# RWKV preparation reordered: small products first, decays beside the receptance, key norms per token

## What is computed

```python
xx = x_prev - x
r = (x + xx * mu[0]) @ w_rkv[0]
xw = x + xx * mu[1]
k = (x + xx * mu[2]) @ w_rkv[1]
v = (x + xx * mu[3]) @ w_rkv[2]
xa = x + xx * mu[4]
xg = x + xx * mu[5]
w_log = -softplus(-(w0 + tanh(xw @ w1) @ w2)) - 0.5
decay = exp(-exp(w_log))
a = sigmoid(a0 + (xa @ a1) @ a2)
g = sigmoid(xg @ g1) @ g2
kk = (k * k_k).reshape(B, S, H, N)
kk = kk / maximum(norm(kk, axis=-1), 1e-12)
k = k * (1.0 + (a - 1.0) * k_a)
# recurrence with state decay w, keys k, values v, removal -kk and kk * a
bonus = sum(rh * kh * r_k, axis=-1) * vh
```

## Time and profile before

| What | us |
|---|---|
| Median of 3 runs | 3485.09 |
| Lowest and highest run | 3481.71, 3485.85 |
| The profiled execution's own time | 3488.07 |
| Its span, first to last instruction | 3486.3 |
| TensorE busy | 3176.3 |
| VectorE busy | 1073.3 |
| ScalarE busy | 1038.5 |
| GpSimd busy | 751.4 |
| Mean granted TensorE clock | 0.946 of full speed |

### The profile page before, as it was taken

The page is one execution under the profiler, slowest core; times in us unless marked ns, Lnnn a source line. Parts: engine busy times, 40 slices in busy tenths (PEclk is TensorE's granted clock), DMA queues, the critical chain, the costliest instruction groups (busy, mean ns, idle before and its releaser), DMA issues.

```text
span 3486.3 us, 39216 instructions
## 1 busy us (share of the span) xinstructions
PE 3176.3 (91%) x16396; PEld 2264.3 (65%) x16396; DVE 1073.3 (31%) x1783; ACT 1038.5 (30%) x1775; POOL 751.4 (22%) x360
## 2 busy tenths in 40 slices
PE   7998999997885888888989999999999999999996
PEld 5676678885553888756768877777788574333332
DVE  4434320214277555653231022415230231000001
ACT  3533432324533221314343232431322031111110
POOL 3122244442220000003234443210144021100001
PEclk9999999998887888989999999999999999999998
DMA  3231143421110000032122322211132138999996
GB/s 113 91 127 61 49 170 108 145 97 36 61 49 1 2 2 2 14 97 91 51 82 97 97 85 97 85 49 49 37 97 88 63 154 367 409 399 413 417 415 274
DMA packets 217630, 447.75 MB, mean 128 GB/s; under 512 B 14176, under 2 KB 191360, under 8 KB 204528
## 3 DMA queue, kind: packets, MB, share of 16 engines
q1 hardware_dynamic: 197664, 389.04, 30.4%
q10 hardware_dynamic: 9744, 36.18, 2.6%
q0 software_dynamic: 10048, 20.02, 1.7%
HBM read 501.82 MB, written 31.46 MB: 153 GB/s over the span
## 4 chain that ended last, share of the span: by engine, by line
PE 80%; DVE 7%; DMA 6%; ACT 3%; issue 2%; POOL 1%; SPq 0%; ACTq 0%; POOLq 0%; DVEq 0%
PE product_banks L580 14%; PE product_banks L581 14%; PE product_banks L582 14%; PE product_banks L2130 7%; PE product_banks L548 5%; PE product_banks L2167 3%; DMA A<-in_w_down 3%; PE product_banks L663 3%; PE product_banks L2604 1%; PE score_banks L1159 1%; PE product_banks L622 1%; PE product_banks L623 1%; PE stat_bank L785 1%; PE stat_bank L701 1%; POOL Wr_parts L485 1%
## 5 line engine op out<-in xcount | busy, mean ns | idle before, releaser
L485 POOL TENSOR_TENSOR Wr_parts<-Wr,Wr_parts 128x1024 fp32r<-128x1024 f32 x202 | 487.1, 2413 | 1203.7 <-ACT Wr_parts L462 1203.7
L581 PE MATMUL product_banks<-A_parts,Wr_parts 128*128 128x512 f32 x1520 | 600.9, 395 | 0.0
L462 ACT ACTIVATE Wr_parts<-Wr 128x1024 fp32r<-128x1024 f32 x202 | 212.8, 1058 | 695.7 <-PE product_banks L582 632.1
L580 PE MATMUL product_banks<-H_parts,Wr_parts 128*128 128x512 f32 x840 | 341.9, 407 | 16.7 <-POOL Wr_parts L485 16.2
L2130 PE MATMUL product_banks<-A,Wr 128*64 128x512 f32 x1312 | 340.6, 597 | 3.4 <-DMA A<-in_w_up 2.2
L582 PE MATMUL product_banks<-H_parts,Wr_parts 128*128 128x512 f32 x840 | 334.2, 398 | 0.0
L581 PEld LDWEIGHTS product_banks<-A_parts,Wr_parts 128*128 128x128 f32 x1520 | 288.7, 190 | 66.3 <-issue 2.4
L485 POOL TENSOR_TENSOR shared_con_parts<-Wr,shared_con_parts 128x1024 fp32r<-128x1024 f32 x80 | 193.5, 2419 | 465.3 <-ACT shared_con_parts L462 465.3
L580 PE MATMUL product_banks<-A_parts,Wr_parts 128*128 128x512 f32 x680 | 268.3, 395 | 23.3 <-DVE A_parts L498 15.6
L582 PE MATMUL product_banks<-A_parts,Wr_parts 128*128 128x512 f32 x680 | 266.3, 392 | 0.0
L2130 PEld LDWEIGHTS product_banks<-A,Wr 128*64 128x64 f32 x1312 | 109.8, 137 | 209.2 <-issue 205.1
(11 more groups left out here) (480 smaller groups left out, 5067.6 us busy)
## 6 DMA issues: line engine op xcount, KB each, us to landing
A<-in_w_down SPq DMA_DIRECT2D x29, 2048.0 KB, 13.6
A<-in_w_gate SPq DMA_DIRECT2D x28, 2048.0 KB, 12.1
A<-in_w_up SPq DMA_DIRECT2D x28, 2048.0 KB, 16.9
Wr<-in_m_w_up SPq DMA_DIRECT2D x32, 1024.0 KB, 5.1
Wr<-in_m_w_down SPq DMA_DIRECT2D x32, 1024.0 KB, 4.9
Wr<-in_w_in SPq DMA_DIRECT2D x32, 1024.0 KB, 5.3
Wr<-in_c_w_kv SPq DMA_DIRECT2D x16, 1024.0 KB, 5.3
expert_rows<-LB ACTq DMA_DIRECT2D x12, 1024.0 KB, 4.0
```

The costliest lines, as they stand in the source:

```text
L462: nc.scalar.activation(weight_parts(s)[0], loaded_part(s), ACT.Copy).then_inc(*mark("weights_high", s))
L485: nc.gpsimd.tensor_tensor(lo, loaded_part(s), hi, ALU.subtract).then_inc(*mark("weights_split", s))
L580: pe.matmul(bank[:, :], hi[:, k, :], x_hi, start=(kk == 0), stop=False)
L581: pe.matmul(bank[:, :], hi[:, k, :], x_lo, start=False, stop=False)
```

## The change

The five small products come first, w1, a1, g1, w2, a2, and then r, k_ and v_ without anything between them, so that they form one run of split weights. The receptance's product is read by VectorE instead of ScalarE and multiplied by its decay in the same step. The decays are scanned before r. The running sum is kept, and the decay up to the token before is read as the neighbouring column instead of being made by a subtraction and an exponential of its own. ScalarE squares the keys straight out of the product's bank.

The key norms are kept per token: a sum for a tile is four matmuls of two columns (`kk_sum_pe`), ScalarE takes the root of 8 columns, VectorE works on 128 x 8 elements (`scale`), and TensorE spreads the scale over the channels again with eight matmuls of 128 columns (`kk_spread_pe`). `prepare` on VectorE finishes one tile of the keys. All this is written between the tiles of k_ and v_, as are the bonus sums and half of the values' turns. Eight bonus sums are copied out of their banks (`keep_sum`).

The core of the diff (removed lines can be seen in the functions above):

```diff
         if "B" in phases:
-            lin("r", a.b_w_rkv[0, 0], D, split=True)
             lin("w1", a.b_w1[0], 64)
+            lin("a1", a.b_a1[0], 64)
+            lin("g1", a.b_g1[0], 128)
             lin("w2", a.b_w2[0], D, k=64)
+            lin("a2", a.b_a2[0], D, k=64)
+            lin("r", a.b_w_rkv[0, 0], D, split=True, evac="dve")
             lin("k_", a.b_w_rkv[0, 1], D, split=True)
-            lin("a1", a.b_a1[0], 64)
-            lin("a2", a.b_a2[0], D, k=64)
...
-        MIX = [(0, "r"), (1, "w"), (2, "k"), (4, "a"), (5, "g"), (3, "v")]
-        LASTMM = {"r": ("r", 7), "w": ("w1", 0), "k": ("k_", 7), "a": ("a1", 0), "v": ("v_", 7),
-                  "g": ("g1", 0)}
+        MIX = [(1, "w"), (4, "a"), (5, "g"), (0, "r"), (2, "k"), (3, "v")]
+        MIX_AT = (48, 0, 16, 24, 8, 16)
...
+        def mix_high_act(act, m, t):
+            if m == 3:
+                act.wait_ge(*at("products_done", ("g1", 0)))
+            high_part(act, (("mix", m), t), MIX_PARTS[m](t)[0], mixbuf(m, t),
+                      [("mix_ready", (m, t))])
...
+            take(act, "w1", lambda j: LW[0:64, :], ACT.Tanh, n=1, rows=64)
             mix_act(act, 2)
+            take(act, "a1", lambda j: LB[0:64, 0, :], ACT.Copy, n=1, rows=64)
             mix_act(act, 3)
+            take(act, "g1", lambda j: LB[:, 1, :], ACT.Sigmoid, n=1)
+            for j in range(8):
+                mix_high_act(act, 3, j)
+                ps = take_product(act, "w2", j)
+                nc.scalar.activation(tile(48 + j), ps[:, :], ACT.Sigmoid, bias=pc("w0", j)).then_inc(
+                    *mark("products_read_by_act", ("w2", j)))
+            take(act, "a2", arena(32), ACT.Sigmoid, "a0")
+            first_highs(act, "r")
             mix_act(act, 4)
+            for j in range(8):
+                act.wait_ge(*at("scanned", j))
+                if j >= 2:
+                    act.wait_ge(*at("products_read_by_dve", ("r", j - 2)))
+                nc.scalar.activation(TMP[:, j % 2, :], tile(48 + j), ACT.Exp, scale=-DECAY).then_inc(
+                    *mark("first_decay_ready", j))
+                mix_high_act(act, 4, j)
+                take_product(act, "r", j)
             mix_act(act, 5)
...
+            def kk_root(j):
+                act.wait_ge(*at("kk_summed", j))
+                nc.scalar.activation(small[:, 48 + 8 * j:56 + 8 * j], B7[:, 8 * j:8 * j + 8],
+                                     ACT.Sqrt).then_inc(*mark("kk_root", j))
+            def decays(j):
+                act.wait_ge(*at("products_read_by_dve", ("r", 7)))
+                if j >= 2:
+                    act.wait_ge(*at("tilde_ready", j - 2))
+                nc.scalar.activation(TMP[:, j % 2, :], tile(48 + j), ACT.Exp, scale=DECAY).then_inc(
+                    *mark("decays_ready", (j, 0)))
+                nc.scalar.activation(tile(48 + j), tile(48 + j), ACT.Exp, scale=-DECAY).then_inc(
+                    *mark("decays_ready", (j, 1)))
+                act.wait_ge(*at("decays_ready", (j, 1)))
+                nc.scalar.activation(Pc[:, j, :], tile(48 + j)[:, CH - 1:T:CH], ACT.Copy).then_inc(
+                    *mark("chunk_decay_ready", j))
+            for j in range(8):
+                ps = take_product(act, "k_", j)
                 if j >= 2:
                     act.wait_ge(*at("kk_summed", j - 2))
+                nc.scalar.activation(SQ[:, j % 2, :], ps[:, :], ACT.Square,
+                                     scale=pc("k_k", j)).then_inc(*mark("kk_square", j))
+                nc.scalar.activation(tile(KT_ + j), ps[:, :], ACT.Copy).then_inc(
+                    *mark("products_read_by_act", ("k_", j)))
+                mix_high_act(act, 5, j)
+                if j:
+                    kk_root(j - 1)
+                if j >= 2:
+                    decays(j - 2)
...
+            for m, name in ((0, "w1"), (1, "a1"), (2, "g1")):
+                product(pe, name, *mixed(m))
+            product(pe, "w2", lambda k: LW[0:64, :], lambda k: [("products_read_by_act", ("w1", 0))])
+            product(pe, "a2", lambda k: LB[0:64, 0, :],
+                    lambda k: [("products_read_by_act", ("a1", 0))])
+            product(pe, "r", MIX_PARTS[3], low_ready(("mix", 3)))
+            def beside_keys(t):
+                if t:
+                    kk_sum_pe(pe, t - 1)
+                if t >= 2:
+                    kk_spread_pe(pe, t - 2)
+            product(pe, "k_", MIX_PARTS[4], low_ready(("mix", 4)), then=beside_keys)
+            def beside_values(t):
+                if t == 0:
+                    kk_sum_pe(pe, 7)
+                if t < 2:
+                    kk_spread_pe(pe, 6 + t)
+                else:
+                    bonus_sum_pe(pe, t - 2)
+                if t >= 4:
+                    value_turn_pe(pe, t - 4, 0)
+            product(pe, "v_", MIX_PARTS[5], low_ready(("mix", 5)), then=beside_values)
+            bonus_sum_pe(pe, 6)
+            for m in range(TT):
+                value_turn_pe(pe, m, 1)
+            bonus_sum_pe(pe, 7)
+            pe.wait_ge(*at("products_read_by_act", ("v_", 7)))
...
+        def kk_sum_pe(pe, j):
+            pe.wait_ge(*at("kk_square", j))
+            if j:
+                pe.wait_ge(*at("kk_root", j - 1))
             for m in range(TT):
+                mm = pe.matmul(B7[:, 8 * j + 2 * m:8 * j + 2 * m + 2],
+                               SQ[:, j % 2, m * P:(m + 1) * P], cc("blk")[:, 0:P:HD],
+                               start=True, stop=True)
+            mm.then_inc(*mark("kk_summed", j))
+        def kk_spread_pe(pe, j):
+            pe.wait_ge(*at("kk_scale_ready", j))
+            if j >= 2:
+                pe.wait_ge(*at("kk_ready", j - 2))
+            for m in range(TT):
+                for e in range(2):
+                    c = 48 + 8 * j + 2 * m + e
+                    mm = pe.matmul(S2[HD * e:HD * e + HD, j % 2, m * P:(m + 1) * P],
+                                   small[:, c:c + 1].broadcast_to([P, HD]), ident,
+                                   start=True, stop=True)
+            mm.then_inc(*mark("kk_spread", j))
+        def bonus_sum_pe(pe, j):
+            pe.wait_ge(*at("bonus_raw", j))
+            if j >= 2:
+                pe.wait_ge(*at("bonus_kept", j - 2))
+            else:
+                pe.wait_ge(*at("kk_ready", 6 + j))
+            pe.matmul(S2[:, j % 2, :], cc("blk"), SQ[:, j % 2, :], start=True, stop=True).then_inc(
+                *mark("bonus_summed", j))
...
             for j in range(8):
+                dve.wait_ge(*at("products_read_by_act", ("w2", j)))
+                nc.vector.tensor_tensor_scan(tile(48 + j), cc("reset"), tile(48 + j), 0.0,
+                                             ALU.mult, ALU.add).then_inc(*mark("scanned", j))
+            mix_dve(dve, 4)
+            for j in range(8):
+                ps = await_product(dve, "r", j)
+                dve.wait_ge(*at("first_decay_ready", j))
+                nc.vector.tensor_tensor(tile(RT_ + j), ps[:, :], TMP[:, j % 2, :], ALU.mult).then_inc(
+                    *mark("products_read_by_dve", ("r", j)))
+                mix_low_dve(dve, 4, j)
+            mix_dve(dve, 5)
+            def scale(j):
+                dve.wait_ge(*at("kk_root", j))
+                v = small[:, 48 + 8 * j:56 + 8 * j]
+                link(dve, nc.vector.tensor_scalar(v, v, 1e-12, None, ALU.max))
+                link(dve, nc.vector.reciprocal(v, v))
+                nc.vector.tensor_scalar(v, v, -1.0, None, ALU.mult).then_inc(
+                    *mark("kk_scale_ready", j))
+            KN = LB[:, 0, :]
+            def prepare(j):
+                k, b, e = tile(KT_ + j), tile(BT_ + j), tile(48 + j)
+                dve.wait_ge(*at("kk_spread", j))
                 dve.wait_ge(*at("products_read_by_act", ("k_", j)))
+                if j:
+                    dve.wait_ge(*at("a_tilde", j - 1))
+                nc.vector.scalar_tensor_tensor(out=KN, in0=k, scalar=pc("k_k", j),
+                                               in1=S2[:, j % 2, :], op0=ALU.mult,
+                                               op1=ALU.mult).then_inc(*mark("kk_ready", j))
+                dve.wait_ge(*at("products_read_by_act", ("a2", j)))
+                nc.vector.tensor_scalar(RS[:, :], b, pc("k_a", j), comp[:, 48 + j:49 + j],
+                                        ALU.mult, ALU.add).then_inc(*mark("k_ready", j))
                 dve.wait_ge(*at("kk_ready", j))
+                nc.vector.scalar_tensor_tensor(out=b, in0=KN, scalar=-1.0, in1=b, op0=ALU.mult,
+                                               op1=ALU.mult).then_inc(*mark("b_ready", j))
+                dve.wait_ge(*at("k_ready", j))
+                link(dve, nc.vector.tensor_tensor(k, k, RS[:, :], ALU.mult))
+                dve.wait_ge(*at("decays_ready", (j, 0)))
+                link(dve, nc.vector.tensor_tensor(b, b, TMP[:, j % 2, :], ALU.mult))
+                nc.vector.tensor_tensor(k, k, TMP[:, j % 2, :], ALU.mult).then_inc(
```

(25 more changed lines are left out.)

250 lines of the change are left out of this document (88 added, 162 removed).

## The result

The changed kernel takes 3448.00 us (median of 4 runs, 3446.26 to 3450.07) against 3483.44 for the kernel before, measured beside it: a ratio of 0.9896 with a 95% interval of 0.9881 to 0.9912. That is 35.4 us less, where 23.6 had been forecast; the time lies in the stated range, between the forecast and its "kinder clock" rival. The profiled execution took 3447.75 us against 3488.07 before, 40.3 less; the execution profiled before lay 4.6 us above its median, the one after lies at it. The traces are compared by these two.

The account below looks back on a forecast made before the run. TensorE was taken as the bound from first mix to grams; its new list, summed in order, put the first mask at 1079.4 instead of 1102.97, a gain of 23.6 us, so 3461.5 us, with 0.8 chance of 3438 to 3476.

Parts of the forecast that it names:

- kinder clock: Rival: 64-row work holds full clock, saving 6.7 us in a2, or the clock survives pauses; one or both, chance 0.28.
- The waits in k_: Beside the keys' product, TensorE stands still 4.0 us for the scale before each of six spreads, 24.0 us together.
- The clock behind a wait: After each of the six pauses in k_ the clock falls, costing 1.9 us more each, 11.4 together.
- w2 and a2: Last two small products before r: 11.0 us taken for w2 and 14.0 for a2, at full clock 7.3.
- The first bonus sum: In v_, TensorE waits 5.8 us for VectorE's last prepare, copy and product, plus 1.9 for the clock.
- The tail: From the end of v_ to the first mask: remaining sums, turns and the grams' start, 9.0 us.
- The pause before r: Between a2 and r, TensorE waits 4.14 us for r's first weight parts, made only after a2's last sigmoid.
- r: The first large product, after the small ones, costs what it cost before, 45.7 us with its cold start.
- The rival's other form: The clock stays up through the pauses, saving 7 x 1.9 = 13.3 us: 3448.2 us; no separate chance given.
- The wait is not there: Rival: scales are ready when TensorE asks in k_, saving 24.0 and 11.4 us: 3426 us; chance 0.05.
- VectorE becomes the bound: Rival beside k_: prepare exceeds its 8.0 us; 3479.5 at 3 us more; chance 0.09, shared with other missed waits.
- slower: Rival: the clock never comes back between waits in k_, perhaps v_ too, up to 3525 us; slow clock's chance 0.06.

Follow-up runs that it names:

- e1: Changed kernel with VectorE's scale of tile j - 2 moved ahead of prepare and the low part of the values' input: 3416.51 us.
- e2: Changed kernel with ScalarE making the high part of the values' input before waiting for that tile of the keys, not after: 3411.17 us.
- e4: Changed kernel with w2 held until ScalarE has made the receptance input's eight high parts, so TensorE pauses before it; products stay at 64 rows: 3465.4 us.
- e5: The pause before w2 as in e4, but w2 and a2 multiplied over 128 rows, the added input rows cleared to zero: 3448.0 us.
- e10: The kernel of e2 run once more, with times: median 3412.95 us of 4 runs.
- e3: Changed kernel with ScalarE making the high part of r's first weight tile after five of a2's eight sigmoids instead of after all: 3444.0 us.
- e8: Changed kernel with the edits of e2 and e3 together and the bonus sums one tile later: 3415.78 us.
- e9: The kernel of e8 run once more, for one profile: 3424.1 us in one run.

## Why the prediction was right, and where its parts were not

- **The waits in k_** were forecast as six of 4.0 us before L2983, released by VectorE behind a low part that ends 0.55 us after GpSimd: there are six of 3.93 and 3.94, and the low part ends 0.54 after it. e1 and e2 took them away from two sides. This was the largest term, and it held.
- **The clock behind a wait** was put at 1.9 us. It fell in all six, and cost 2.3: 1.4 in the products and 0.9 because the spread itself (1.97 instead of 1.09 us) ran at half clock. I had priced the spread at full clock though it stands right behind the pause. Over six rounds that is 2.7 us more than the 11.4 of the sum; k_ came to 92.4 against 90.9, and 1.4 of it fell into v_'s first tile, where I had none.
- **w2 and a2** were the step that failed: "For a2 I take 14.0, what w2 took", and 11.0 for w2. They took 14.1 together, not 25.0, which is 10.9 of the 16.4 us by which the first mask came early (1063.0, not 1079.4). The row behind it was read rightly, its clock never came back in 14.01 us; but that row shows a product that began cold, and in the new order w2 begins hot. The same trace had a hot case, the first half of a2 at 0.92 us a tile (3.67 us for four), and I took only its second half. e4 and e5 show what a cold start does, with 64 rows and with 128. The rule that I cited there (the Trainium skill, TensorE: Matmul & The Clock Gate, Part 1), by which sustained activity of any shape releases the clock, gave the right 7.3 for a2, but not for its reason: e4's 27.7 us of sustained 64-row work at 0.50 contradict it.
- **The first bonus sum** waits 1.79 us, not 5.8. `prepare` of the last tile was there (1014.92), but of two holds by GpSimd one came, of 1.5 us, and the copy took 0.43 instead of 0.7. The clock did not fall, which saved another 1.9; that was luck, since behind the same wait it fell in e10. v_ is 56.9 instead of 61.0.
- **The tail** is 7.2 instead of 9.0, because ScalarE's copies kept pace. **The pause before r** is 4.45 against 4.1, w1 with a1 and g1 23.6 against 24.1, **r** 45.5 against 45.7, and the stage began 0.75 early.
- Added up: -0.75 - 0.5 - 10.9 + 0.35 - 0.2 + 1.5 - 4.1 - 1.8 = -16.4. The rest of the change is as it was argued: the small products joined, the tail emptied, most of that eaten by k_. By the profiled executions 40.3 us came instead of 23.6, by the medians 35.4. So the range held, but the gain was 1.5 times the forecast, and nearly all the errors lay on one side.
- **The rivals.** "The clock is kinder" was half right: kinder to a2, not to the pauses. That half, priced at 6.7 us, misses the 3.9 of w2. The rival's other form, in which the clock stays up through the pauses, had 3448.2 us, almost the measured 3448.0; that is chance, for in all six pauses of k_ the clock fell. "The wait is not there", "VectorE becomes the bound" and "slower" did not come; in e1, where the waits are gone, VectorE is at once the bound.

## What to carry to other kernels

Before a small result is waited for, read what stands ahead of its making on each engine: three operations of 0.2 us cost 37 us here because they stood behind one that waited for something else, and moving one line on either engine gives most of it back. Put products of few rows behind dense ones, not behind a pause. When an engine is freed of waits, ask what it collides with next, and when an order is changed to dodge a collision, look at the instruction behind it too.

## What the hardware showed that I had not expected

- w2 and a2, products of 64 rows, hold the full clock (14.1 us in the changed kernel) and do not win it back (27.7 us at 0.50 in e4), while the same with 128 rows had it back within 4.3 us (e5). Grams of 64 rows, in pairs on both halves, did win it back.
- A hold by GpSimd takes small instructions of VectorE on SBUF alone as well as large ones: a copy of 16 columns took 2.39 us, a multiplication of 8 columns 2.16, where they take 0.18 and 0.17. An instruction that reads PSUM is not held (L3055, 0.75 us beside GpSimd), nor is a reciprocal on SBUF alone. In the kernel before one took the same 3.35 us beside GpSimd as elsewhere:

```profile
303.18 4.68 POOL L485 TENSOR_TENSOR Wr_parts<-Wr,Wr_parts 128x1024 fp32r<-128x1024 f32 x2 [29.05 <-ACT Wr_parts L462]
...
305.60 3.35 DVE L719 RECIPROCAL SC<-SC 128x512 f32<-128x512 f32 x1 [16.17 <-ACT SC L713]
```

- A pause of 1.79 us left the clock alone in six of the seven profiles that had it, and not in e10; one of 2.2 us was followed by 0.50 in all three that had it (e3, e8, e9).
- The same code behind the first mask took between 1794.2 us (e5) and 1810.2 (e9) up to the experts, by the clock granted in the recurrence. So of changes ahead of it some 7 us, and 13 in one profile, can be lost without a cause in their own stage.
